# Norm outputs transposed by DMA instead of TensorE; gains and residuals of the norms applied elsewhere

## The reference

```python
def rmsnorm(x, g):
    xf = x.astype(jnp.float32)
    y = xf * lax.rsqrt(jnp.mean(xf * xf, axis=-1, keepdims=True) + EPS) * g.astype(jnp.float32)
    return y.astype(x.dtype)

def layer(...):
    xn = rmsnorm(x, g_pre_mix)
    z = xn @ w_in                                     # (B,T,6144)
    xa, ga, u, v, gates = jnp.split(z, [...], axis=-1)
    # branch A: RG-LRU
    xc, conv_new = causal_conv(xa, conv_prev, conv_w, conv_b)
    hseq, h_last = rglru(xc, h0, w_a, b_a, w_x, b_x, lam)
    o_a = (hseq * jax.nn.gelu(ga)) @ w_br_a
    # branch B: gMLP spatial gating
    vn = layernorm(jax.nn.gelu(v), ln_g, ln_b)
    o_b = (jax.nn.gelu(u) * spatial_gate(vn, w_s, b_s)) @ w_br_b
    # gated merge + single output projection
    g_a, g_b = jnp.split(jax.nn.sigmoid(gates), 2, axis=-1)
    mix = (g_a * o_a + g_b * o_b) @ w_out
    x = x + rmsnorm(mix, g_post_mix)
    # SwiGLU channel mixer
    hn = rmsnorm(x, g_pre_ffn)
    gate, up = jnp.split(hn @ w_ffn_in, 2, axis=-1)
    f = (jax.nn.silu(gate) * up) @ w_ffn_out
    return x + rmsnorm(f, g_post_ffn), h_last, conv_new, vn
```

## Time and profile before

| what | value |
|---|---|
| median of the runs shown | 2220.86 us (2218.76 to 2222.97) |
| the profiled execution's own time | 2213.88 us |
| its span (slowest core, core 7) | 2212.0 us |
| the eight cores' spans in it | 2196.0 to 2212.0 us |
| granted TensorE clock, mean of a core | 0.981 to 0.984 |
| TensorE busy | 2072.7 us, 94% |
| VectorE busy | 1155.9 us, 52% |
| ScalarE busy | 907.0 us, 41% |
| GpSimd busy | 547.5 us, 25% |

### The profile page before, as it was taken

How to read it: one execution, slowest core, us unless ns; L and a number is a source line. 1 busy time by engine, 2 the same in 40 slices (tenths; PEclk the granted TensorE clock), 3 DMA queues, 4 the chain that set the end, 5 groups by cost and what they waited for, 6 DMA issues and landing times.

```text
span 2212.0 us, 34961 instructions; the slowest of 8 cores (2196.0 to 2212.0 us)
## 1 busy us (share of the span) xinstructions
PE 2072.7 (94%) x10666; PEld 1013.4 (46%) x10666; DVE 1155.9 (52%) x1790; ACT 907.0 (41%) x1537; POOL 547.5 (25%) x887
## 2 busy tenths in 40 slices
PE   4899799997999999999999999999999999899998
PEld 2344344443444444444444454455555555455453
DVE  5747734257622586137842485248527725673343
ACT  3836512348213571228512471247137423641311
POOL 2234211524104410044003320232033023212310
PEclk9899999998999999999999999999999999999999
DMA  9798798984999657773546454565684676365563
GB/s 185 153 194 185 142 187 178 225 230 106 210 214 248 213 148 192 203 243 111 184 150 212 159 191 157 175 225 210 201 263 152 231 218 224 115 218 181 185 208 100
DMA packets 117704, 416.11 MB, mean 188 GB/s; under 512 B 14537, under 2 KB 14545, under 8 KB 117522
## 3 DMA queue, kind: packets, MB, share of 16 engines
q1 hardware_dynamic: 97362, 341.48, 46.4%
q0 software_dynamic: 20016, 72.36, 20.5%
q10 hardware_dynamic: 144, 0.05, 0.0%
HBM read 432.62 MB, written 53.54 MB: 220 GB/s over the span
## 4 chain that ended last, share of the span: by engine, by line
PE 79%; DMA 8%; DVE 5%; issue 3%; POOL 3%; ACT 2%; DVEq 0%; POOLq 0%; SPq 0%; ACTq 0%
PE ps L709 55%; PE ps L1236 13%; DMA wring<-wall 4%; PE ps L954 4%; PE ps L1140 3%; DMA wring<-wsc 2%; DVE xcf L830 1%; DMA wsc<-wring 1%; PE ps L661 1%; PE ps L1249 1%; PE ps L848 1%; POOL stats L640 1%; PE ps L1016 1%; POOL x L1164 1%; DVE xcf L826 1%
## 5 line engine op out<-in xcount | busy, mean ns | idle before, releaser
L709 PE MATMUL ps<-hnT,wring 128*128 128x512 bf16 (+2 forms) x3168 | 634.8, 361 | 19.2 <-DMA wring<-wall 5.9
L709 PE MATMUL ps<-xnT,wring 128*128 128x512 bf16 (+2 forms) x2880 | 614.3, 365 | 36.0 <-DMA wring<-wall 11.7
L709 PEld LDWEIGHTS ps<-hnT,wring 128*128 128x128 bf16 x3168 | 309.7, 98 | 333.2 <-issue 34.0
L709 PEld LDWEIGHTS ps<-xnT,wring 128*128 128x128 bf16 x2880 | 279.9, 99 | 324.3 <-issue 70.7
L1236 PE MATMUL ps<-wring,ffT 128*128 128x512 bf16 (+1 forms) x1364 | 299.6, 381 | 2.5 <-DMA wring<-wall 2.5
L1215 ACT ACTIVATE sgt<-ps 128x512 f32<-128x512 f32 (+2 forms) x198 | 109.4, 554 | 384.0 <-PE ps L709 353.8
L1219 DVE SCALAR_TENSOR_TENSOR sgt<-sgt,ps 128x512 f32<-128x512 f32 (+2 forms) x198 | 125.3, 633 | 189.6 <-PE ps L709 184.6
L1236 PEld LDWEIGHTS ps<-wring,ffT 128*128 128x128 bf16 (+1 forms) x1364 | 132.9, 98 | 165.4 <-issue 9.4
L1104 DVE SCALAR_TENSOR_TENSOR ffT<-ffT,ps 128x512 f32<-128x512 f32 (+1 forms) x122 | 75.8, 632 | 212.8 <-PE ps L709 182.2
L830 DVE SCALAR_TENSOR_TENSOR xcf<-xa,vecs_sb,xcf 128x512 f32<-128x512 f32 (+2 forms) x240 | 164.8, 687 | 25.8 <-DVE xcf L830 0.5
L475 POOL DMA_DIRECT2D wring<-wall x139 | 78.0, 563 | 400.4 <-PE ps L709 285.5
(11 more groups left out here) (148 smaller groups left out, 2092.0 us busy)
## 6 DMA issues: line engine op xcount, KB each, us to landing
wring<-wsc SPq DMA_DIRECT2D x475, 512.0 KB, 4.7
wring<-wall POOLq DMA_DIRECT2D x137, 512.0 KB, 9.7
wsc<-wring SPq DMA_DIRECT2D x68, 512.0 KB, 8.7
xin<-xp SPq DMA_DIRECT2D x30, 512.0 KB, 7.0
x<-xp SPq DMA_DIRECT2D x29, 512.0 KB, 7.1
yp<-x SPq DMA_DIRECT2D x29, 512.0 KB, 6.8
wring<-wsc SPq DMA_DIRECT2D x16, 256.0 KB, 3.4
yp<-xin SPq DMA_DIRECT2D x4, 256.0 KB, 2.0
```

The source lines that it names most:

```text
L709: mm(lambda e, k=k: e.matmul(ps[:, b, 0:nt], lhsT=wv[:, k, m * 128:(m + 1) * 128], rhs=rhsT[:, k, 0:nt], start=(k == 0), stop=(k == NCH - ...
```

## The change

- **Transposition.** `norm_T` becomes one `dma_start_transpose` per sub-tile, issued on ScalarE's queue: 128 tokens x 1024 bf16 (256 KB) from the corner of `ffT` straight into `xnT` or `hnT`. The eight matmuls, the PSUM bank, the VectorE evacuation and the stages `xte` and `hte` are gone; the identity matrix too. There are 66 of them.
- **Gains of the pre-norms.** As the transposition can no longer multiply, `norm_scale` now multiplies by 1/rms and by the gain, token-major, in one VectorE instruction; the gains lie in two new buffers `gbc_qm`, `gbc_qf`, spread over all partitions by DMA (512 KB each, the first one at the very start on ScalarE's queue). ScalarE no longer scales.
- **Post-norms.** The gain is multiplied in place in PSUM by VectorE while 1/rms is being made; then one VectorE instruction multiplies by 1/rms and adds x. The buffer `tok` and GpSimd's additions are gone. `ev0` multiplies with the gain while it leaves PSUM; its squares are taken from PSUM.
- **Small.** The factor 32 = sqrt(1024) moves from the gains into the squares (`scale=1/32`), the epsilons with it; `spe` works in place in PSUM; `vout` uses the other half of `gv`.
- **Planner.** Transfers on ScalarE's queue get a clock of their own, 3.3 ns a KB for 512 KB, twice that if the DMA queue is busy.

The core of the diff:

```diff
+            if eng == "act":
+                self.act_dma = max(self.act_dma, start) + kb * self.DMA_NS * (2 if busy else 1)
+                o.end = self.act_dma + self.DMA_LAT
...
             def su_vecs():
+                cdma(lambda e: e.dma_start(out=gbc_qm[:], in_=rows_in[R_GQM].partition_broadcast(128)), writes=[("gbc_qm",)], kb=512)
...
             def norm_sq(src, PT, cells, xb):
                 ss = stat()
-                act(lambda e: e.activation(out=xb[0][0:PT, :], in_=src, func=AF.Square, accum_out=stats[0:PT, ss:ss + 1]),
+                act(lambda e: e.activation(out=xb[0][0:PT, :], in_=src, func=AF.Square, scale=1.0 / 32, accum_out=stats[0:PT, ss:ss + 1]),
...
+            def norm_scale(src, PT, cells, r, xb, gain, gcell):
+                dve(lambda e: e.scalar_tensor_tensor(out=xb[0][0:PT, :], in0=src, scalar=stats[0:PT, r:r + 1], in1=gain[0:PT, :],
+                                                     op0=ALU.mult, op1=ALU.mult), 1024, cells + [("st", r), gcell], xb[1])
+
+            def norm_T(xb, PT, col, dstT, dcell, sm):
+                dma("act", lambda e: e.dma_start_transpose(dstT[:, :, col:col + PT], xb[0][0:PT, :]), sm, 512, xb[1], [dcell])
...
-                    put("xtr", ("xtr", t, s), lambda s=s: xtr(s), needs=lambda s=s: c_xsb(s), pe=True, nb=1,
+                    put("xtr", ("xtr", t, s), lambda s=s: xtr(s), needs=lambda s=s: c_xsb(s), idle=lambda s=s: [("xnT", s)],
                         after=[("xsc", t, s)] + ([("ma", t - 1, 7)] if prev else []))
...
-                    G["pnr", s] = rstd(ss, PT, 4.0 * D * EPS)
+                    G["pnr", s] = rstd(ss, PT, 4.0 * EPS)
+                    for n in range(2):
+                        dve(lambda e, n=n: e.tensor_tensor(out=ps[0:PT, pr + n, :], in0=ps[0:PT, pr + n, :],
+                                                           in1=gbc_pm[0:PT, n * 512:(n + 1) * 512], op=ALU.mult), 512,
+                            [("ps", pr + n), ("gbc_pm",)], [("ps", pr + n)])
...
-                    pool(lambda e: e.tensor_tensor(
-                        out=xflat[s][0:PT, n * 512:(n + 1) * 512], in0=xflat[s][0:PT, n * 512:(n + 1) * 512], in1=tok[0:PT, tk, :], op=ALU.add), 512,
-                        cells_x[s] + [("tok", tk)], cells_x[s])
+                    half = slice(n * 512, (n + 1) * 512)
+                    dve(lambda e: e.scalar_tensor_tensor(out=xflat[s][0:PT, half], in0=ps[0:PT, b, :], scalar=stats[0:PT, r:r + 1],
+                                                         in1=xflat[s][0:PT, half], op0=ALU.mult, op1=ALU.add), 512,
+                        cells_x[s] + [("ps", b), ("st", r)], cells_x[s])
...
                 def ev0(s):
-                    dve(lambda e: e.tensor_copy(out=fh0[0:PT, s, :], in_=ps[0:PT, b, :]), 512, [("ps", b)], [("gvh", s // 2, s % 2)])
+                    G["ss0", s] = sq_half(s, b)
+                    dve(lambda e: e.tensor_tensor(out=fh0[0:PT, s, :], in0=ps[0:PT, b, :], in1=gbc_pf[0:PT, 0:512], op=ALU.mult), 512,
+                        [("ps", b), ("gbc_pf",)], [("gvh", s // 2, s % 2)])
...
-                ("pe", "hnt xtr gate out xa sup sp mg mx v ga u f"),
-                ("act", "pna hna hnb xcb xae gev gex sqrt sig fia ve gae ue xsq xsc fa su_decay"),
-                ("dve", "hte xte pnb brx fie gin scan cv ln ln2 vb spe ev0 fb su_gates su_spat"),
+                ("pe", "gate out xa sup sp mg mx v ga u f"),
+                ("act", "hnt xtr pna hna xcb xae gev gex sqrt sig fia ve gae ue xsq fa su_decay"),
+                ("dve", "pnb hnb brx fie gin scan cv ln ln2 vb spe xsc ev0 fb su_gates su_spat"),
```

## The result

The changed kernel took 2376.9 us (2376.0 and 2377.8), 1.070 times the kernel before, with a 95% interval of 1.066 to 1.075: 156 us slower, where 14 had been forecast. That lies between the rival of late transfers (2,275 us) and that of a transposition at a small part of a copy's rate (2,590 us).

A forecast was written before the change was run, and what follows sets the result against it. TensorE, busy 94%, was taken as the bound. Boundaries +43.6 us, less 15.0 and 14.7 for removed transpositions, made +13.9 us: 2,235 us, 0.6% slower, range 2,195 to 2,280 us.

The forecast's parts named there:

- the rival of late transfers: Transpositions land late, 15.3 us at tile boundaries (11.5 for three sub-tiles): +54 us, 2,275 us; chance 17%.
- a small part of a copy's rate: Each transposition takes 15.3 us, one after another, 61 us per boundary: some 2,590 us from boundaries alone; chance 4%.
- The bound and the removed work: TensorE, busy 94%, bounds the kernel; removing 66 transposition sets gains 29.7 us, boundary waits included.
- Four issues at the 0.64 us that SyncE's four took: At t = 4 and t = 8 the last sigmoid queues behind ScalarE's four issues: stalls of 2.1 and 2.9 us.
- The last part: Closing signs of error: landing outside 3 to 14 us, issues holding ScalarE much over 0.64 us, short stretches changing over 10 us.
- the fillers: At boundaries, 24 or 16 remaining merge matmuls, 5.16, 3.44 or 2.58 us, run while the transpositions land.
- My eight stalls: TensorE waits at the eight tile boundaries, 2.1 to 6.6 us each, 32.4 us in sum.
- The clock: After stalls over 2.3 us TensorE runs slower: 1.6 us more at each of seven boundaries, 11.2 us.
- Start: nothing, at worst a few us: First tile: xnT comes 2 to 8 us later, but TensorE waits 7.6 us on weights at 41 us anyway.
- hnT: Other matmuls cover transfers except in the first two tiles; put at nothing, +5 us each as the bad end.
- VectorE and GpSimd: Over the kernel VectorE's work rises some 75 us and GpSimd's falls some 165 us, both far from the bound.
- The rival of the freed engines: Stretches from 200 and 500 us win back 29.5 us: 2,205 us, or 2,167 with quick landing; chance 7%.

The follow-up runs named there:

- e2: The changed kernel with only the first tile's four xnT transpositions back on TensorE, the rest by DMA on ScalarE's queue: 1.055 of the kernel before, 2,342 us.
- e3: The changed kernel with all xnT transpositions on TensorE and all 33 hnT transpositions by DMA: 1.0025 of the kernel before, 2,226 us.
- e1: The changed kernel with all 66 transpositions back on TensorE, plain VectorE copy out of PSUM, rest of the change kept: 0.989 of the kernel before, 2,197 us.
- e6: The changed kernel with the first tile's xnT on TensorE and the other 62 transpositions issued by SyncE: 1.028 of the kernel before, 2,283 us.
- the bf16 version with GpSimd's queue: The changed kernel, but the first weight loads, still issued by GpSimd, read one bf16 block instead of f32 weights (left out of the result): 2,306.5 us.
- e7: The changed kernel with first tile's xnT on TensorE and, from the third tile, xnT transposed earlier into a second buffer: 1.084 of the kernel before, 2,408 us.
- e4: The changed kernel with each tile's xnT transpositions issued only after the last sigmoid of the merge ahead: 1.081 of the kernel before, 2,400 us.
- e5: The changed kernel with no weight load issued before the first tile's four transpositions have landed: 1.052 of the kernel before, 2,337 us.

## Why the prediction was wrong, step by step

Taken apart by the ratios, the 156 us are: the first tile's xnT 35 (the change less e2), the other eight xnT 115 (e2 less e3), hnT 30 (e3 less e1), the rest of the change -24 (e1 less before). The last two hang on e1 and are known to some 20 us.

**The bound and the removed work: right.** TensorE's busy time fell by 12 us, where the sets at 0.45 us each had made 27.6 with the waits left out; what lowers that is the slow clock behind the stalls (hgT alone rose from 123.6 to 138.4 us).

**The step that failed first: "Four issues at the 0.64 us that SyncE's four took".** I had priced the issue of a transposition by the issue of a copy. It took 1.25 us at least, for xnT 2.2 us in the median, and up to 28.4 us beside the first f32 loads. What sets its length stays open. The number of packets is a near guess, 1,056 for 256 KB (4,224 for the four of a tile) and some 150 for a copy of 512 KB (342.00 MB in 97,506), but it does not set the floor: the decode sub-tile of 64 tokens has 544 (3,712 for the four of t = 8) and its xnT issue still took 1.27 to 1.31 us on all eight cores of the change. The row of the quantity that I needed, the hold of ScalarE, did not exist in the trace of before, and I bounded it from above with nothing but the issue of a copy. The last part had named this as the point where it would fail: "if an issue holds ScalarE much longer than 0.64 us, so that work queued behind it comes late".

**The second: who waits.** I let the sigmoid behind the issues matter at t = 4 and t = 8 alone, because at the others the fillers (hgT and gsT matmuls) were to run while the transfers landed. But the fillers are merge matmuls, and the last of them waits itself for that sigmoid. With the measured hold the term comes out: at t = 3, 9.4 for the issues, 0.6 for the sigmoid and 0.6 for the handovers, less the 1.65 us that the matmuls under way still took, are the 8.95 us measured. My eight stalls were 32.4 us, measured 68 (61 and 7) on this core; for the sigmoid alone the other cores waited 66 to 80 us. With ScalarE free (e6), the wait for the landing appears that I had forecast, but 54 us of it; so the landing was undersized too, and the two costs lie over one another.

**The follow-up costs were mis-sized.** The clock cost about what I had put (14.8 us of hgT against 11.2). Beside it, e2 waits 41.5 us for weights in front of the projections where e3 waits 27.8, and 51.8 us for hnT where e3 waits 31.0. I had no term for that; that stalls and slow landings push transfers into one another is a reading. These are the slowest core of each; over the eight cores of e2 the wait for hnT goes from 11 to 52 us. With the wait for the sigmoid (68.9 against 7.0) this is 96 of the 130 us that xnT of eight boundaries cost before the 15 us saved; the rest, the clock among it, I cannot assign.

**"Start: nothing, at worst a few us": wrong**, by 30 to 70 us on the eight cores, of which 35 reached the end. I knew the stretch as saturated, and let TensorE's wait for weights at 41 us hide a transfer of 2 to 8 us. From the first issue to the first matmul it was 37 to 76 us.

**hnT: the place was right, the size not.** The first two tiles lose, as I wrote, but 20 and 9.5 us instead of nothing, or 5 at the bad end; a later one, which I had as covered, waits 3.9 us.

**VectorE and GpSimd:** +33 us instead of +75, -136 instead of -165; neither bounds the kernel. The rival of the freed engines was true in part: the rest of the change brings 24 us. I had given it 7% and taken for it only the case in which the transpositions cost nothing.

**The range.** The two ends came from copies, and the upper one was misread: 15.3 us was the landing of one copy in a list of medians, while in the same trace a load of weights took up to 29.7 us. The rival "a small part of a copy's rate" was the right kind for the start, and its 4% too little; it was put down for every transposition, while landings one after another at that rate (up to 56.2 us) came only at the start, beside f32 loads. By the block figure of the Trainium skill's page "VectorE: DVE Perf Modes" (The three transpose paths), eight blocks of 1,309 ns would be an estimated 10.5 us for a sub-tile; the quickest landing in the changed kernel's profile was 2.9 us, so the trace does not bear it out for a stream of blocks. The Trainium skill's page "Advanced Engine Details and Errata" (X-Bar Transpose (TRN2)) states that transposing transfers are as fast as regular ones. The trace disagrees: 17.61 MB on ScalarE's queue, nearly all transpositions, took 7.3% of the engines' time, 342.00 MB of copies on SyncE's queue 43.3%, so 3.3 times as much for a byte, the slow start included; in the bf16 version with GpSimd's queue, where the start is quick, it is 2.0 times (18.13 MB in 5.1%, 342.00 MB in 47.4%).

## What to carry to other kernels

Price the issue of a transfer by a measured issue of the same kind beside the same traffic, not by another kind's, and look who stands behind it on the issuing engine: here ScalarE, with work in its queue, was held for 1.25 to 28 us by each. A transposition that a bound engine does in 1.8 us, at a place where the other engines' work for it is due at once, is not worth a DMA; where much other work covers it, DMA and TensorE were equal. Issuing it sooner (e7) or behind the work that it held up (e4) gained nothing here, and from SyncE (e6) gave back the hold but left 98 us of waiting for landings, so look first at what shares the DMA engines with it.

## What the runs showed of the hardware

- A DMA transposition of 128 x 1024 bf16 made 1,056 packets, nearly all of 256 bytes. With little beside it (e5) the issue took 1.25 us and it landed 3.1 to 3.5 us after the issue; with ordinary copies beside it (the change from 1,020 us on, slowest core) 1.25 to 5.5 us and 2.9 to 18.5 us.
- Beside the first f32 loads that are turned into bf16 one issue lasted 22.4 to 28.4 us on each of the eight cores, and the first matmul came at 52.7 to 91.2 us. On the worst core traffic fell to 29 GB/s for 30 us and a packet took 0.47 us; on five cores there was no such fall (191 to 221 GB/s, 0.025 to 0.046 us).
- The engine that issues a transposition is held meanwhile: up to 28.4 us by one on ScalarE, up to 11.6 us by one on SyncE (e6, where the first tile's xnT is not among them).
